# The tail's seven-product feed-forwards: VectorE's order at the entry, TensorE's first products, and the adding up of the banks are rebuilt

## The chip, the cores and the metric

One core of a Trainium2 chip runs the whole program in one launch. The metric is the device time in microseconds of that core, the median of several runs; less is better.

## The reference, cut to what matters

Two transformer blocks of depth 2 follow one another over 256 tokens of width 1024. The change touches the second one, called the tail here, whose two layers (A and B) each end in the same feed-forward and normalisation:

```python
def sq_relu_mlp(x, w1, w2):
    return jnp.square(jax.nn.relu(x @ w1)) @ w2

def layer_norm(x, g, b):
    mu = jnp.mean(xf, axis=-1, keepdims=True)
    var = jnp.mean(jnp.square(xf - mu), axis=-1, keepdims=True)
    ...
...
        x = layer_norm(ALPHA * x + sq_relu_mlp(x, mlp_w1[i], mlp_w2[i]), ln_ffn_g[i], ln_ffn_b[i])
```

`w1` is 1024 x 4096, `w2` is 4096 x 1024, all in f32. ALPHA is the square root of 2.

## The kernel before, in words

**Digits.** Large products are not done on f32 operands. Each operand is split into a high and a low part in the type fp32r. ScalarE writes the high part as a copy (`w_hi`, `hid_hi`, `s_hi`, `t_hi`), VectorE the low part as the f32 value less the high part (`w_lo`, `hid_lo`, `s_lo`, `t_lo`), and TensorE adds up three products (high times low, low times high, high times high).

**Tiles.** The weights of a feed-forward come as 16 tiles of 2 MB: `ff1.0` to `ff1.7` hold 512 columns of `w1` each, `ff2.0` to `ff2.7` the 512 rows of `w2` that go with them. They rotate through three ring buffers, in the order ff1.0, ff1.1, ff2.0, ff1.2, ff2.1 and so on. SyncE loads a tile when TensorE has given its buffer back (`tile_used`). The low part is written over the f32 tile in the ring.

**Seven products.** In A and B, `ff2.0` to `ff2.6` are multiplied with a scheme of seven products in place of eight: activations (two halves of tokens) and weights (two halves of rows, two halves of columns) are combined by sums and differences first. `dve_form_sums` makes four sums of weights (`t_sum`, L1353), `dve_hidden_sums` four sums of activations (L1373 to L1378), `dve_form_lows` the low parts (L1365) in four steps: 0 for the left columns (`col_hi`, shown as w_hi_work), 1 for the right columns (`right_hi`, shown as w_hi_big), 2 and 3 for two of the sums (`t_hi`). `dve_hidden_first` is the low part of the first token half (L1386), `dve_hidden_sums_low` that of the sums (L1398). The seven results grow in seven banks of PSUM over the seven tiles: banks 1 to 7. One of the seven products, that of bank 6, is done in f32 without digits (four matmuls a tile). `ff2.7` is done in the usual way by `ff2(7)`, in four quarters `q` of 12 matmuls each (token half, column half), which land in banks 4 to 7.

**Order on TensorE.** After `ff1(1)`, which makes the hidden blocks 2 and 3 in bank 0 and bank 1, tile `ff2.0` is multiplied: `seven_first(0)`, `seven_second(0)`, `seven_rest(0)`. `seven_first` and `seven_second` are low times high and high times high into banks 4 and 1, and need `hid_lo`; `seven_rest` begins with high times low into the same two banks. Then, for n from 2 to 7: half of `ff1.n` (`ff1_unit(n, 0)`, 48 matmuls), `seven_first(n-1)`, the other half (`ff1_unit(n, 1)`, 48 matmuls), `seven_second(n-1)`, `seven_rest(n-1)`. All units from n = 2 on write bank 0, so each waits until ScalarE has taken the one before out of it (relu, L1317). At the end `ff2(7)`.

**Order on VectorE.** An order written out by hand in `dve_mlp_seven` (L1400): sums of weights, step 0, sums of activations, first low part, step 1, low part of the sums, steps 2 and 3; then for each n the low halves of the next `ff1` tile (`lower_columns`, L1270), and the same again. `dve_seven_products` (L1426) then waits for the last matmul of bank 6 (`seven_done`) and adds the banks into `x` with ten instructions, after which the layer norm (L2959) adds the quarters of `ff2(7)` one by one (L2918) as they come.

**Order on ScalarE.** `act_mlp_seven` (L1309): `hidden(f)` is relu, square and high part of one hidden block (L1317 to L1321), `act_hidden_forms` the high part of the sums (L1307), `act_split` the high parts of the next tile (L1233), `act_column_forms` and `act_right_forms` those of the weights (L1290 to L1302). `form_used` counts four times a tile: TensorE is done with `col_hi`, bank 7, bank 3, bank 2.

**After A**, TensorE turns token half 0 of the normalised `x` (L522) in the last quarter of `ff2(7)`, between its sixth and seventh matmul. After B, the normalised rows are stored and the program ends.

Of the kernel before, what the change touches and what calls it, by code (L numbers as in the profile page):

```python
# [14 lines left out]
P = 128  # L15
S = 256
# [280 lines left out]
def program(nc, ctx, I, out):  # L297
# [169 lines left out]
    hid_turned = sig("hid_turned")  # L467
    t_summed, form_hi, form_lo = sig("t_summed"), sig("form_hi"), sig("form_lo")
    s_summed, s_high, s_low = sig("s_summed"), sig("s_high"), sig("s_low")
    form_used = sig("form_used")  # L470
    seven_done, seven_read = sig("seven_done"), sig("seven_read")
    hid_rows = [hT[:, 2 * t:2 * t + 2, :].rearrange("p k t -> p (k t)") for t in range(TT)]
    ff2_ready, ff2_saved = sig("ff2_ready", 4), sig("ff2_saved", 4)
    stored = sig("stored")
# [14 lines left out]
    def mlp_nth(pre):  # L489

        return 1 if pre == "B." else 0
# [13 lines left out]
    def pe_kit(pe, st, wide_, aux_, tiles, splits, places):  # L505
# [141 lines left out]
        def mlp(pre, turns, between=None, second_token=None, between_at=3, last_turn=None):  # L647
# [91 lines left out]
            def seven_first(n):  # L739

                m, s = seventh(pre, n), 4 * (n % 2)
                pe.wait_ge(form_hi.sem, st.at(form_hi, DIGIT_FORMS * m + 1))
                pe.wait_ge(hid_lo_ready.sem, st.at(hid_lo_ready, FB // 2 * mlp_nth(pre) + 2 * n + 2))
                for o, v in ((bank[4], 1), (bank[1], 0)):
                    if n == 0 and v == 0:
                        pe.wait_ge(wide_.saved.sem, st.at(wide_.saved, wide_.nth_save(f"{pre}f3")))
                    for u in range(2 if v else 1):
                        f = s + 2 * u + v
                        mm(o, hid_lo[:, f, 0:P], col_hi[:, u, v, :], n == 0 and u == 0, False)
                        mm(o, hid_hi[:, f, 0:P], col_hi[:, u, v, :], False, False)  # L750

            def seven_second(n):

# [4 lines left out]
            def seven_rest(n, lo):  # L758

                m, s = seventh(pre, n), 4 * (n % 2)  # L760
                w, first, final = blocks(lo), n == 0, n == LAST - 1
                pe.wait_ge(form_lo.sem, st.at(form_lo, DIGIT_FORMS * m + 1))
                for o, v in ((bank[4], 1), (bank[1], 0)):
                    for u in range(2):
                        mm(o, hid_hi[:, s + 2 * u + v, 0:P], w[:, u, v, 0:BANK], False, final and u == 1 and v == 0)
# [12 lines left out]
                by_digits(bank[3], 1, t_hi[0], t_lo[0], final, form_used)  # L778
                if DIGIT_SUMS > 1:
                    pe.wait_ge(form_lo.sem, st.at(form_lo, DIGIT_FORMS * m + 4))  # L780
                    by_digits(bank[2], 3, t_hi[1], t_lo[1], final, form_used)
                else:
                    pe.wait_ge(t_summed.sem, st.at(t_summed, 4 * m + 3))
                    for u in range(2):
                        mm(bank[2], s_form(sums_, 3, u), t_sum[1][:, u, :], first and u == 0, final and u == 1,
                           form_used if u == 1 else None)
                pe.wait_ge(t_summed.sem, st.at(t_summed, 4 * m + 4))
                for u in range(2):
                    mm(bank[6], hid_f[:, s + 2 * u + 1, P:S], t_sum[2][:, u, :], first and u == 0, False,
                       seven_done if final and u == 1 else None)  # L790

            def seven_open(n):

# [27 lines left out]
            if pre in SEVEN:  # L821
                ff1(1)
                lo = seven_open(0)
                seven_first(0)
                seven_second(0)
                seven_rest(0, lo)
                tile_done()
                for n in range(2, LAST + 1):
                    w = next_columns(f"{pre}ff1.{n}")
                    ff1_unit(n, 0, w)  # L830
                    lo = seven_open(n - 1)
                    seven_first(n - 1)
# [476 lines left out]
    def act_mlp_seven(st, act, wide_, pre, tiles, splits):  # L1309
# [29 lines left out]
        act_split(st, act, tiles, splits, f"{pre}ff2.{LAST}", (0,))  # L1339
        hidden(2 * LAST + 1)  # L1340
        act_split(st, act, tiles, splits, f"{pre}ff2.{LAST}", (1,))

    def dve_form_sums(st, dve, tiles, pre, n):

# [55 lines left out]
    def dve_mlp_seven(st, dve, pre, tiles, splits):  # L1400

        dve_form_sums(st, dve, tiles, pre, 0)
        dve_form_lows(st, dve, tiles, pre, 0, (0,))
        dve_hidden_sums(st, dve, pre, 0)
        dve_hidden_first(st, dve, pre, 0)
        dve_form_lows(st, dve, tiles, pre, 0, (1,))
        dve_hidden_sums_low(st, dve, pre, 0)
        dve_form_lows(st, dve, tiles, pre, 0, range(2, DIGIT_FORMS))
        for n in range(1, LAST):
            ahead = f"{pre}ff1.{n + 1}"  # L1410
            lower_columns(st, dve, tiles, splits, ahead, 0)
# [14 lines left out]
    def dve_seven_products(st, dve, pre):  # L1426

        half = [[x[:, t, c * BANK:(c + 1) * BANK] for c in range(2)] for t in range(TT)]

        def scaled(o, b):  # L1430
            dve.scalar_tensor_tensor(out=o, in0=o, scalar=ALPHA, in1=b, op0=ALU.mult, op1=ALU.add).then_inc(st.up(dve_step), 1)  # L1431

        def added(o, a, b, signal=dve_step):
            dve.tensor_tensor(o, a, b, ALU.add).then_inc(st.up(signal), 1)

        dve.wait_ge(seven_done.sem, st.at(seven_done, mlp_nth(pre) + 1))
        scaled(half[0][1], bank[7])
        scaled(half[1][1], bank[7])
        scaled(half[0][0], bank[1])
        scaled(half[1][0], bank[3])  # L1440
        dve.tensor_copy(y_sum, bank[1]).then_inc(st.up(dve_step), 1)
        dve.wait_ge(st.last.sem, st.reached())
        added(y_sum, y_sum, bank[2])
        dve.wait_ge(st.last.sem, st.reached())
        added(half[0][1], half[0][1], y_sum)
        added(half[1][0], half[1][0], y_sum)
        added(y_sum, y_sum, bank[3])
        dve.wait_ge(st.last.sem, st.reached())
        added(half[1][1], half[1][1], y_sum, seven_read)

    def hidden_pairs(name):

# [2067 lines left out]
```

## Time and profile before

| | |
|---|---|
| median of 3 runs | 1466.64 us |
| the three runs | 1464.3, 1466.64, 1479.1 us |
| the profiled execution's own time | 1466.25 us |
| its span in the profile | 1464.4 us |
| TensorE matmul busy | 1430.8 us (98%) |
| VectorE busy | 953.8 us (65%) |
| ScalarE busy | 772.3 us (53%) |
| GpSimd busy | 289.3 us (20%) |

Times in the profile are from the span's start. The feed-forward of A takes about 985 to 1169 us, that of B 1274 to 1462 us. A matmul's row shows its start and a modelled length; matmuls overlap, so the distance between starts is the cadence. Idle time stands in square brackets behind an instruction, with what ended it.

### The profile page before, as it was taken

To read this page: it belongs to the slowest core of one execution; us is meant where nothing else is said; L and a number is where in the kernel's file an instruction comes from. 1 tells how busy PE (TensorE), PEld (TensorE's weight loads), DVE (VectorE), ACT (ScalarE), POOL (GpSimd) and SP (SyncE) were. 2 spreads that over 40 slices of the span, in tenths; PEclk is the share of its full clock that TensorE was granted. 3 is DMA by queue.
4 is the path that set the end of the run, shared out by engine and by line. 5 is a ranking of instruction groups with operands and counts; after the bars stand their busy time and mean duration, and the time that the engine had idled before them with its cause. 6 is when DMAs were issued, how large, how long until landed. Compare 5 with 4: busy or idle time off the path is not lost.

```text
span 1464.4 us, 20055 instructions
## 1 busy us (share of the span) xinstructions
PE 1430.8 (98%) x8528; PEld 1212.3 (83%) x8528; DVE 953.8 (65%) x1170; ACT 772.3 (53%) x952; POOL 289.3 (20%) x109
## 2 busy tenths in 40 slices
PE   7999999999999999999999999999999999999997
PEld 5788889998877788888989788688888788888886
DVE  5337764454553364854444669878998857589987
ACT  4565626544455554654455366647666336276662
POOL 4598140000029694410000000000000004000000
PEclk9999999999999999999999999999999999999999
DMA  8833345654446543445566353315565453255551
GB/s 303 298 133 127 117 154 192 219 209 176 174 156 235 195 147 116 166 169 212 174 195 219 126 185 112 107 60 182 192 228 176 151 197 115 73 205 187 198 210 49
DMA packets 121224, 250.28 MB, mean 171 GB/s; under 512 B 15040, under 2 KB 27056, under 8 KB 121008
## 3 DMA queue, kind: packets, MB, share of 16 engines
q1 hardware_dynamic: 120872, 248.90, 48.5%
q8 instruction: 68, 1.11, 0.3%
q14 instruction: 20, 0.16, 0.0%
q10 hardware_dynamic: 264, 0.10, 0.0%
HBM read 247.94 MB, written 1.05 MB: 170 GB/s over the span
## 4 chain that ended last, share of the span: by engine, by line
PE 88%; DVE 8%; ACT 2%; POOL 1%; issue 1%; DMA 0%; DVEq 0%; ACTq 0%
PE psum L515 84%; PE psum L522 4%; POOL w_lo L1263 1%; DVE x L2924 1%; DVE w_lo L1270 1%; DVE big L2918 1%; ACT w_hi_big L1299 0%; DVE tiny L2967 0%; DVE x L1431 0%; DMA work<-in_norm_mix 0%; DVE rows L1731 0%; DVE t_lo L1365 0%; DVE w_lo L1365 0%; DVE w_lo L1263 0%; DVE x L2918 0%
## 5 line engine op out<-in xcount | busy, mean ns | idle before, releaser
L515 PE MATMUL psum<-ht_hi,w_lo 128*128 128x256 f32 x960 | 275.6, 287 | 4.9 <-ACT work L1317 3.8
L515 PE MATMUL psum<-w_lo,ht_hi 128*128 128x512 f32 (+1 forms) x576 | 222.4, 389 | 0.9 <-DVE w_lo L1263 0.9
L515 PEld LDWEIGHTS psum<-ht_hi,w_lo 128*128 128x128 f32 x960 | 181.5, 189 | 10.8 <-issue 9.7
L515 PE MATMUL psum<-w_lo,hid_hi 128*128 128x512 f32 x344 | 129.2, 395 | 0.0
L515 PEld LDWEIGHTS psum<-w_lo,ht_hi 128*128 128x128 f32 x576 | 108.3, 188 | 22.4 <-DVE w_lo L1263 1.7
L515 PE MATMUL psum<-ht_lo,w_hi_rows 128*128 128x256 f32 x448 | 126.4, 282 | 0.0
L515 PE MATMUL psum<-ht_hi,w_hi_rows 128*128 128x256 f32 x448 | 126.2, 282 | 0.0
L515 PE MATMUL psum<-ht_lo,w_hi_tmp 128*128 128x256 f32 x448 | 125.1, 279 | 0.0
L515 PE MATMUL psum<-ht_hi,w_hi_tmp 128*128 128x256 f32 x448 | 124.8, 279 | 0.0
L1263 POOL TENSOR_TENSOR w_lo<-ring,w_hi_work 128x2048 fp32r<-128x2048 f32 x12 | 57.4, 4784 | 254.1 <-ACT w_hi_work L1243 254.1
L1243 ACT ACTIVATE w_hi_work<-ring 128x2048 fp32r<-128x2048 f32 x26 | 49.7, 1913 | 81.4 <-PE psum L515 78.8
L515 PE MATMUL psum<-hT,ring 128*128 128x256 f32 (+2 forms) x480 | 89.8, 346 | 0.0
L515 PEld LDWEIGHTS psum<-ht_lo,w_hi_tmp 128*128 128x128 f32 x448 | 85.2, 190 | 3.5 <-issue 2.9
L515 PEld LDWEIGHTS psum<-ht_lo,w_hi_rows 128*128 128x128 f32 x448 | 86.8, 194 | 0.4
L515 PEld LDWEIGHTS psum<-hT,ring 128*128 128x128 f32 (+1 forms) x480 | 78.2, 186 | 10.5 <-issue 2.4
L515 PEld LDWEIGHTS psum<-ht_hi,w_hi_rows 128*128 128x128 f32 x448 | 85.3, 190 | 0.0
L1263 POOL TENSOR_TENSOR w_lo<-ring,w_hi_big 128x2048 fp32r<-128x2048 f32 x3 | 13.7, 4567 | 359.3 <-DVE work L2918 359.3
L515 PEld LDWEIGHTS psum<-ht_hi,w_hi_tmp 128*128 128x128 f32 x448 | 83.9, 187 | 0.0
L515 PEld LDWEIGHTS psum<-w_lo,hid_hi 128*128 128x128 f32 x344 | 64.6, 188 | 15.2 <-issue 0.5
L1529 DVE TENSOR_TENSOR hid_lo<-work,hid_hi 128x512 fp32r<-128x512 f32 x32 | 22.1, 692 | 83.6 <-ACT hid_hi L1503 83.6
L1263 DVE TENSOR_TENSOR w_lo<-ring,w_hi_work 128x2048 fp32r<-128x2048 f32 x15 | 34.4, 2292 | 62.9 <-ACT w_hi_work L1243 62.9
L1263 DVE TENSOR_TENSOR w_lo<-ring,w_hi_tmp 128x2048 fp32r<-128x2048 f32 x24 | 55.0, 2291 | 24.6 <-ACT w_hi_tmp L1243 24.6
(440 smaller groups left out, 3752.0 us busy)
## 6 DMA issues: line engine op xcount, KB each, us to landing
ring<-in_w_ff SPq DMA_DIRECT2D x32, 2048.0 KB, 8.0
ring<-in_mlp_w SPq DMA_DIRECT2D x32, 2048.0 KB, 8.4
ring<-in_w_in SPq DMA_DIRECT2D x19, 2048.0 KB, 7.8
ring<-in_w_out SPq DMA_DIRECT2D x4, 2048.0 KB, 8.1
ring<-in_w_ple_gate SPq DMA_DIRECT2D x4, 2048.0 KB, 8.0
ring<-in_sb_ssm_w_in SPq DMA_DIRECT2D x4, 2048.0 KB, 8.4
ring<-in_dsa_w_in SPq DMA_DIRECT2D x3, 2048.0 KB, 8.0
ring<-in_w_up_nsa SPq DMA_DIRECT2D x2, 2048.0 KB, 8.4
```

The costliest lines, as they stand in the source:

```text
L515: ins = pe.matmul(o, lhsT, rhs, start=start, stop=stop)
L522: ins = pe.transpose(o, in_, ident[0:n, 0:n])
L1243: act.activation(w_hi[place][:, 0:width], ring[n % RING][:, h * width:(h + 1) * width], ACT.Copy) \
L1263: eng.tensor_tensor(w_lo[n % RING][:, c], ring[n % RING][:, c], w_hi[places[name][h]][:, 0:width].bitcast(F32), ALU.subtract) \
L1270: dve.tensor_tensor(w_lo[n % RING][:, :].rearrange("p (k n) -> p k n", k=KT)[:, :, c], ring[n % RING][:, :].rearrange("p (k n) -> p k n", ...
L1529: dve.tensor_tensor(lo, h, hi.bitcast(F32), ALU.subtract).then_inc(st.up(hid_lo_ready), 1)
L2918: return dve.tensor_tensor(o, a, b, op)
L2924: return dve.scalar_tensor_tensor(out=o, in0=a, scalar=s1, in1=b, op0=op0, op1=op1)
```

## The change

It does three things, in A and in B alike:

1. VectorE does steps 1 and 2 of `dve_form_lows` for `ff2.0` ahead of the sums of activations; step 3 stays behind the low part of the sums.
2. `seven_first(0)`, `seven_second(0)` and the first four matmuls of `seven_rest(0)` become `seven_entry`: the same twelve matmuls in another order. Eight that need only `hid_hi` (high times high, high times low) come first, the four that need `hid_lo` last. The wait for ScalarE's relu of hidden block 3 (it frees bank 1) now stands behind the first four.
3. `dve_seven_products` waits per bank (`form_used` 2, 3 and 4) in place of waiting for `seven_done`, which is gone; the copy of bank 1 moves from VectorE to ScalarE (`y_copied`); `seven_read`, for which quarter 3 of `ff2(7)` waits, is signalled after the second instruction in place of the last.

```diff
+            def seven_entry(lo):
+                w, m = blocks(lo), seventh(pre, 0)
+                pe.wait_ge(hid_hi_ready.sem, st.at(hid_hi_ready, FB // 2 * mlp_nth(pre) + 2))
+                pe.wait_ge(form_lo.sem, st.at(form_lo, DIGIT_FORMS * m + 1))
+                for o, v in ((bank[4], 1), (bank[1], 0)):
+                    if v == 0:
+                        pe.wait_ge(wide_.saved.sem, st.at(wide_.saved, wide_.nth_save(f"{pre}f3")))
+                    for u in range(2):
+                        mm(o, hid_hi[:, 2 * u + v, 0:P], col_hi[:, u, v, :], u == 0, False)
+                        mm(o, hid_hi[:, 2 * u + v, 0:P], w[:, u, v, 0:BANK], False, False)
+                pe.wait_ge(hid_lo_ready.sem, st.at(hid_lo_ready, FB // 2 * mlp_nth(pre) + 2))
+                for o, v in ((bank[4], 1), (bank[1], 0)):
+                    for u in range(2):
+                        mm(o, hid_lo[:, 2 * u + v, 0:P], col_hi[:, u, v, :], False, False, form_used if v == 0 and u == 1 else None)
...
-                seven_first(0)
-                seven_second(0)
+                seven_entry(lo)
                 seven_rest(0, lo)
...
+        act.wait_ge(form_used.sem, st.at(form_used, 4 * seventh(pre, LAST - 1) + 2))
+        act.activation(y_sum, bank[1], ACT.Copy).then_inc(st.up(y_copied), 1)
...
         dve_form_sums(st, dve, tiles, pre, 0)
         dve_form_lows(st, dve, tiles, pre, 0, (0,))
+        dve_form_lows(st, dve, tiles, pre, 0, (1, 2))
         dve_hidden_sums(st, dve, pre, 0)
         dve_hidden_first(st, dve, pre, 0)
-        dve_form_lows(st, dve, tiles, pre, 0, (1,))
         dve_hidden_sums_low(st, dve, pre, 0)
-        dve_form_lows(st, dve, tiles, pre, 0, range(2, DIGIT_FORMS))
+        dve_form_lows(st, dve, tiles, pre, 0, range(3, DIGIT_FORMS))
...
-        dve.wait_ge(seven_done.sem, st.at(seven_done, mlp_nth(pre) + 1))
+        used = 4 * seventh(pre, LAST - 1)
+        dve.wait_ge(form_used.sem, st.at(form_used, used + 2))
         scaled(half[0][1], bank[7])
-        scaled(half[1][1], bank[7])
+        dve.scalar_tensor_tensor(out=half[1][1], in0=half[1][1], scalar=ALPHA, in1=bank[7], op0=ALU.mult, op1=ALU.add) \
+            .then_inc(st.up(seven_read), 1)
+        dve.wait_ge(form_used.sem, st.at(form_used, used + 3))
+        scaled(half[1][0], bank[3])
+        dve.wait_ge(y_copied.sem, st.at(y_copied, mlp_nth(pre) + 1))
         scaled(half[0][0], bank[1])
-        scaled(half[1][0], bank[3])
-        dve.tensor_copy(y_sum, bank[1]).then_inc(st.up(dve_step), 1)
-        dve.wait_ge(st.last.sem, st.reached())
+        dve.wait_ge(form_used.sem, st.at(form_used, used + 4))
         added(y_sum, y_sum, bank[2])
...
-        added(half[1][1], half[1][1], y_sum, seven_read)
+        added(half[1][1], half[1][1], y_sum)
+        dve.wait_ge(st.last.sem, st.reached())
```

## Rows read from the trace of the kernel before

**Rows 1.** The page's part 4, the chain that ended last: shares by engine.
```profile
PE 88%; DVE 8%; ACT 2%; POOL 1%; issue 1%; DMA 0%; DVEq 0%; ACTq 0%
```
**Rows 2.** Waits of TensorE, 990 us to the end: total us, times, longest.
```profile
PE psum L515 <- ACT work L1317: 3.8, 2, 1.9
PE psum L522 <- DVE x L2924: 1.9, 1, 1.9
PE psum L515 <- DVE hid_lo L1386: 0.6, 2, 0.3
```
**Rows 3.** Timeline, VectorE, entry of A: start us, length us, instruction, idle before.
```profile
1002.64 2.29 DVE L1365 TENSOR_TENSOR w_lo<-ring,w_hi_work 128x2048 fp32r<-128x2048 f32 x1
...
1008.82 0.42 DVE L1373 TENSOR_TENSOR work<-work 128x256 f32<-128x256 f32 x1 [3.88 <-ACT hid_hi L1463]
...
1014.54 2.35 DVE L1365 TENSOR_TENSOR t_lo<-big,t_hi 128x1024 fp32r<-128x1024 f32 x2
1016.81 2.29 DVE L1270 TENSOR_TENSOR w_lo<-ring,w_hi_tmp 128x2048 fp32r<-128x2048 f32 x1
```
**Rows 4.** Timeline, ScalarE, entry of A.
```profile
1010.53 1.06 ACT L1307 ACTIVATE s_hi<-work 128x1024 fp32r<-128x1024 f32 x1
1011.50 0.58 ACT L1317 ACTIVATE work<-psum 128x512 f32<-128x512 f32 x1
...
1013.32 1.90 ACT L1233 ACTIVATE w_hi_tmp<-ring 128x2048 fp32r<-128x2048 f32 x1
...
1030.49 0.58 ACT L1317 ACTIVATE work<-psum 128x512 f32<-128x512 f32 x1
```
**Rows 5.** Timeline, VectorE, entry of B.
```profile
1292.95 2.29 DVE L1365 TENSOR_TENSOR w_lo<-ring,w_hi_work 128x2048 fp32r<-128x2048 f32 x1
1298.25 0.42 DVE L1373 TENSOR_TENSOR work<-work 128x256 f32<-128x256 f32 x1 [3.01 <-ACT hid_hi L1463]
...
1306.24 2.29 DVE L1270 TENSOR_TENSOR w_lo<-ring,w_hi_tmp 128x2048 fp32r<-128x2048 f32 x1
```
**Rows 6.** Timeline, ScalarE, entry of B.
```profile
1302.74 1.90 ACT L1233 ACTIVATE w_hi_tmp<-ring 128x2048 fp32r<-128x2048 f32 x1
```
**Rows 7.** Timeline, TensorE, entry of A and the first two rounds of its loop.
```profile
1014.68 0.50 PE L515 MATMUL psum<-w_hi_big,s_lo 128*128 128x512 f32 x1 [0.24 <-DVE s_lo L1398]
...
1031.21 0.35 PE L515 MATMUL psum<-ht_hi,w_lo 128*128 128x256 f32 x1 [1.90 <-ACT work L1317]
...
1038.46 0.40 PE L515 MATMUL psum<-w_hi_work,hid_lo 128*128 128x512 f32 x1
...
1054.24 0.28 PE L515 MATMUL psum<-ht_hi,w_lo 128*128 128x256 f32 x1
...
1059.88 0.40 PE L515 MATMUL psum<-w_hi_work,hid_lo 128*128 128x512 f32 x1
```
**Rows 8.** Busy time and granted clock (PEclk) of one stretch after A's wait.
```profile
1033.00:1036.00 3.00, 3.00 (x20) 3.00 (x20) 3.00 (x3) 1.20 (x1) 0.00 (x0) 0.68 0.00 0
```
**Rows 9.** Timeline, TensorE: two other gaps, at the start and at A's end.
```profile
18.14 0.73 PE L515 MATMUL psum<-w_lo,ht_hi 128*128 128x512 f32 x2 [0.94 <-DVE w_lo L1263]
...
1166.14 1.32 PE L522 MATMUL psum<-const,x 128*128 128x128 f32 x8 [1.90 <-DVE x L2924]
```
**Rows 10.** Busy time and granted clock of the stretches behind those two gaps.
```profile
18.00:20.00 2.00, 1.22 (x5) 0.73 (x5) 1.80 (x4) 2.00 (x2) 0.04 (x1) 1.00 1.05 386
...
1168.00:1170.00 2.00, 2.00 (x15) 1.58 (x14) 1.97 (x4) 0.00 (x0) 0.00 (x0) 1.00 0.00 0
```
**Rows 11.** Timeline, VectorE, the ends of A and of B.
```profile
1162.21 0.67 DVE L2918 TENSOR_TENSOR x<-x,psum 128x512 f32<-128x512 f32 x1
...
1438.98 2.29 DVE L1263 TENSOR_TENSOR w_lo<-ring,w_hi_rows 128x2048 fp32r<-128x2048 f32 x1 [1.12 <-ACT w_hi_rows L1243]
1443.96 2.48 DVE L1431 SCALAR_TENSOR_TENSOR x<-x,psum 128x512 f32<-128x512 f32 x4 [2.68 <-PE psum L515]
...
1451.66 0.67 DVE L2918 TENSOR_TENSOR x<-x,psum 128x512 f32<-128x512 f32 x1
```
**Rows 12.** Timeline, TensorE, last matmul of quarter 1 of `ff2(7)`, A and B.
```profile
1159.66 0.40 PE L515 MATMUL psum<-w_hi_rows,hid_hi 128*128 128x512 f32 x1
...
1449.12 0.40 PE L515 MATMUL psum<-w_hi_rows,hid_hi 128*128 128x512 f32 x1
```

More of the change, by code:

```diff
@@ L469, in program @@
     s_summed, s_high, s_low = sig("s_summed"), sig("s_high"), sig("s_low")
-    form_used = sig("form_used")
-    seven_done, seven_read = sig("seven_done"), sig("seven_read")
+    form_used, seven_read, y_copied = sig("form_used"), sig("seven_read"), sig("y_copied")
     hid_rows = [hT[:, 2 * t:2 * t + 2, :].rearrange("p k t -> p (k t)") for t in range(TT)]
@@ L744, in seven_first @@
                 for o, v in ((bank[4], 1), (bank[1], 0)):
-                    if n == 0 and v == 0:
-                        pe.wait_ge(wide_.saved.sem, st.at(wide_.saved, wide_.nth_save(f"{pre}f3")))
                     for u in range(2 if v else 1):
                         f = s + 2 * u + v
-                        mm(o, hid_lo[:, f, 0:P], col_hi[:, u, v, :], n == 0 and u == 0, False)
+                        mm(o, hid_lo[:, f, 0:P], col_hi[:, u, v, :], False, False)
                         mm(o, hid_hi[:, f, 0:P], col_hi[:, u, v, :], False, False)
+            def seven_entry(lo):
[12 more added lines that the diff above has]
+                        mm(o, hid_lo[:, 2 * u + v, 0:P], col_hi[:, u, v, :], False, False, form_used if v == 0 and u == 1 else None)
             def seven_second(n):
@@ L761, in seven_rest @@
                 w, first, final = blocks(lo), n == 0, n == LAST - 1
[L762 to L765, printed above, removed]
+                if not first:
+                    pe.wait_ge(form_lo.sem, st.at(form_lo, DIGIT_FORMS * m + 1))
+                    for o, v in ((bank[4], 1), (bank[1], 0)):
+                        for u in range(2):
+                            mm(o, hid_hi[:, s + 2 * u + v, 0:P], w[:, u, v, 0:BANK], False, final and u == 1 and v == 0)
                 sh, sl, sums_ = s_hi[n % 2], s_lo[n % 2], s_sum[n % 2]
@@ L788, in seven_rest @@
                 for u in range(2):
-                    mm(bank[6], hid_f[:, s + 2 * u + 1, P:S], t_sum[2][:, u, :], first and u == 0, False,
-                       seven_done if final and u == 1 else None)
+                    mm(bank[6], hid_f[:, s + 2 * u + 1, P:S], t_sum[2][:, u, :], first and u == 0, False)
             def seven_open(n):
@@ L1431, in scaled, with added @@
             dve.scalar_tensor_tensor(out=o, in0=o, scalar=ALPHA, in1=b, op0=ALU.mult, op1=ALU.add).then_inc(st.up(dve_step), 1)
-        def added(o, a, b, signal=dve_step):
-            dve.tensor_tensor(o, a, b, ALU.add).then_inc(st.up(signal), 1)
-        dve.wait_ge(seven_done.sem, st.at(seven_done, mlp_nth(pre) + 1))
+        def added(o, a, b):
+            dve.tensor_tensor(o, a, b, ALU.add).then_inc(st.up(dve_step), 1)
+        used = 4 * seventh(pre, LAST - 1)
+        dve.wait_ge(form_used.sem, st.at(form_used, used + 2))
         scaled(half[0][1], bank[7])
-        scaled(half[1][1], bank[7])
+        dve.scalar_tensor_tensor(out=half[1][1], in0=half[1][1], scalar=ALPHA, in1=bank[7], op0=ALU.mult, op1=ALU.add) \
[3 more added lines that the diff above has]
+        dve.wait_ge(y_copied.sem, st.at(y_copied, mlp_nth(pre) + 1))
         scaled(half[0][0], bank[1])
-        scaled(half[1][0], bank[3])
-        dve.tensor_copy(y_sum, bank[1]).then_inc(st.up(dve_step), 1)
-        dve.wait_ge(st.last.sem, st.reached())
+        dve.wait_ge(form_used.sem, st.at(form_used, used + 4))
         added(y_sum, y_sum, bank[2])
```

## The prediction

> **What bounds the kernel now.** I read the chain that ended last first: 88% of it is TensorE [rows 1], so a change on VectorE or ScalarE can only give what TensorE waits for, or what lies behind its last matmul. The second view, TensorE's waits from 990 us to the end, is therefore short and nearly complete [rows 2]: 3.8 us for the relu at L1317 in two waits of 1.9, 1.9 us for the layer norm's last step, 0.6 us for `hid_lo`. In the 474 us of that stretch hardly anything else is to be had.
>
> The timelines then say who stands behind each wait. At A's entry VectorE idles 3.88 us before the sums of activations and has no gap after them [rows 3]; ScalarE's relu at 1030.49 us comes only when VectorE has fed it, and TensorE starts at 1031.21 [rows 4, 7]. B repeats it (idle 3.01 us) [rows 5]. At the ends VectorE idles 2.7 us until the last seven-product matmul, and only then begins ten instructions that most of the banks were ready for [rows 11].
>
> A third view adds a cost that no wait shows. Behind the 1.90 us gap the granted clock is 0.68 over 1033 to 1036 us, partly at the lower of its two levels, 1.2 in place of 2.4 GHz [rows 8]. The 48 matmuls of that unit take 1038.46 - 1031.21 = 7.25 us, those of the next round 1059.88 - 1054.24 = 5.64 us [rows 7]: the lower clock costs 1.6 us in A. B has the same gap, and I take the same price.
>
> **Part 1, steps 1 and 2 of the low parts into the idle time.** One step of the right columns takes 2.2 us (the 2.29 us of the same shape, less the overlap of rows), a step of a sum half of 2.27 us, 1.14 [rows 3]: 3.34 us move.
> - A: step 0 ends at 1004.9 us, so the moved work ends at 1008.3, and the sums still start at 1008.82 [rows 3]. Cost nothing; cover 3.88 us, of which 0.5 is left.
> - B: step 0 ends at 1295.2, the moved work at 1298.5; the sums start 0.25 us later than at 1298.25 [rows 5].
> - Behind the sums VectorE reaches the next tile's low half (L1270) earlier. It was at 1016.81 in A. Now the low part of the sums starts when ScalarE's `s_hi` is done (1010.53 + 1.06 = 1011.6), ends at 1012.8, step 3 at 1013.9. But ScalarE's high half for L1270 is ready only at 1013.32 + 1.90 = 1015.2 [rows 4]. So of 3.34 us only 1016.81 - 1015.25 = **1.56 us** come through. This is what is late next: ScalarE's order, not VectorE's.
> - B: 1302.74 + 1.90 + 0.25 = 1304.9 against 1306.24, **1.33 us** [rows 5, 6].
> - From there to the relu of block 4 the two engines hand work to each other without slack, so the relu and TensorE's restart move by the same amount.
>
> **Part 2, TensorE's order at the entry.** The first product no longer waits for `hid_lo` (0.32 us in each entry, half of 0.6 [rows 2]), and the 0.24 us before 1014.68 goes too, since `s_lo` is ready at 1012.8 [rows 7]. The new wait stands after four matmuls, for the relu of block 3 (1011.50 + 0.58 = 1012.1 [rows 4]); four matmuls at some 0.235 us from 1011.0 end at 1011.9, so it costs 0.2 us in A and, with B's 0.25 us, some 0.4 there. Queued behind it are eight entry matmuls and the whole first tile. TensorE gains about 0.65 us in A and 0.4 in B, and waits them out again at the relu of block 4: worth **nothing** by itself. The order of products within a bank changes no duration.
>
> The gap at that relu becomes 1.90 - 1.56 + 0.65 = 1.0 us in A and 1.90 - 1.33 + 0.4 = 1.0 in B.
>
> **The clock.** No operation in the trace tells what a 1.0 us gap does here; the bounds are no fall (gain 1.6 us each) and the same fall (0). Nearest is the gap of 0.94 us at 18.14, behind which the granted clock stays at 1.00; even A's end with 1.90 us keeps 1.00 [rows 9, 10]. I take no fall: **2 x 1.6 = 3.2 us**. The Trainium skill (TensorE: Matmul & The Clock Gate, "Why this matters for your kernels") lets the clock fall only behind idle stretches longer than any here; by that page the 1.6 us would not be there before, and the sum would come to 6.9 us, or 1459.4. The trace disagrees with it: 0.68 stands behind 1.90 us of idling [rows 8].
>
> **Part 3, the adding up.** Before, ten instructions start at 1443.96 and the layer norm's second addition (quarter 1) at 1451.66 [rows 11]. Now VectorE starts when it has the low half behind it, 1438.98 + 2.29 = 1441.3. Banks 7, 3 and 2 are done by then or within 1 us: behind bank 2 come only four f32 matmuls before 1443.9, and a bank takes six at 0.235 us. ScalarE's copy of bank 1, taken at the relu's 0.58 us for the same shape [rows 4], runs during bank 3; the cover is bank 3's and bank 2's 2.8 us. If that cover is gone, it costs VectorE up to its own old copy, some 0.6 us. Nine instructions at 0.62 to 0.7 us, 5.9 us, end at 1447.2. Before, they ended at 1450.3; 3.1 us are free. Now what is late is quarter 1: its last matmul ends at 1449.12 + 0.40 = 1449.5 [rows 12], so the second addition starts at 1449.56 in place of 1451.66: **2.1 us** of the 3.1 come through at B's end, and the rest of the norm follows unchanged (quarter 3 ends 5.6 us after quarter 1, just ahead of its addition).
> In A the same step moves from 1162.21 to 1159.66 + 0.40 + 0.05 = 1160.1, by 2.1 us [rows 11, 12]. There TensorE's turn is bounded by its own arrival, so the gain is the wait, **1.9 us** [rows 2, 9]. The earlier `seven_read` is hidden: quarter 3 starts at about 1452.3, 2 us after the old signal.
>
> No DMA is issued by a moved step; SyncE's loads follow TensorE and move with it.
>
> **Sum.** 1.56 + 1.33 + 3.2 + 1.9 + 2.1 = 10.1 us against the profiled execution's 1466.25 us (span 1464.4 and 1.85 around it): **1456.2 us**. That execution lies 0.4 us under the median of the runs shown; the runs spread from 1464.3 to 1479.1, so I let 1.5 us stand for the spread.
>
> **Rivals.**
> - *The clock still falls* behind the 1.0 us gaps. For: it fell behind both 1.90 us gaps at this place. Against: [rows 9, 10]. Once: 1457.8; twice: 1466.25 - 6.9 = 1459.4.
> - *The entry gives nothing*, because ScalarE is the bound there, not VectorE: its high halves and the column copies may keep their times. For: half of the moved 3.34 us is already lost to it. Against: between 1015.2 and the relu at 1030.49 ScalarE has less to do than the time holds. Only the ends count: 1466.25 - 4.0 = 1462.3.
> - *Slower.* The moved steps now stand between `hid_hi` and the sums. If ScalarE's right copy came only at the end of the idle time (3.9 us later in A, 3.0 in B), the full 3.34 us would delay `s_hi`, the high halves and the relu: in A 3.34 - 1.56 = 1.8 us lost, in B 3.34 - 1.33 = 2.0, together what the ends give (4.0), with gaps of over 3 us and, if the slow stretch doubles with the gap, 1.6 us more in each: 1466.25 + 3.8 - 4.0 + 3.2 = 1469.3. It decides from about 3 us of lateness. Against: VectorE's step 0 in A starts at 1002.64 without a wait [rows 3]; nothing points to a late copy.
> - *The ends don't move*, since the per-bank signals come with the last one or another instruction holds VectorE: 1466.25 - 6.1 = 1460.1. Against: each signal is tied to its own bank's last matmul.
>
> **Chances.** Forecast 0.57; clock falls once or twice 0.2; entry nothing 0.08; ends don't move 0.06; slower 0.03; the rest a better case, such as an earlier step of ScalarE, or a shifted measurement. The range takes the forecast less 2.7 us (spread, and a clock that stays up elsewhere) and reaches over the clock's case and the entry's: 1453.5 to 1462.5. About 1% (14.7 us) is what a measurement of this kernel can tell from no change; no case but a gain half as large again reaches it. Faster by over 1%: 0.03; within 1%: 0.94; slower by over 1%: 0.03.
>
> **What would show it.** In the changed kernel's trace: L1365 twice more before L1373, whose idle is then under 0.6 us; L1270 some 1.5 us sooner behind L1373 than before; TensorE's wait for L1317 near 1.0 us twice; granted clock 1.00 behind both; no wait at A's L522; L1431 starting some 2.6 us before the last f32 matmul ends, and VectorE waiting for TensorE before quarter 1's addition. The prediction is wrong if the relu's wait keeps 1.9 us, if the clock falls behind a shorter gap, or if a wait at bank 1 of over 0.5 us shows at the entry.

## The result, and the profile after

The changed kernel takes 1456.34 us (median of 20 runs, 1455.5 to 1473.34), the kernel before 1478.82 us beside it (20 runs, 1464.19 to 1496.05); ratio 0.9898, 95% interval [0.9868, 0.9928]. The forecast of 1456.2 us is met to 0.1 us, and still the change in the medians, 22.5 us, is more than twice the 10.4 us that I forecast from the shown 1466.64. That the time itself is met so closely is partly luck: runs of one level spread by some 3 us in either kernel.

The runs, put in order, say why. Those of before fall on levels: nine at 1464.19 to 1466.64, ten at 1478.74 to 1482.91, one at 1496.05. Eighteen runs of the changed kernel lie at 1455.5 to 1458.83, two at 1470.8 and 1473.34. Between the lower levels (medians 1465.5 and 1456.1) lie **9.4 us**; the rest is that 11 of 20 runs of before and 2 of 20 after were on an upper one, so that one median lay up there and the other did not. The profiled execution after is itself an upper one: 1473.34 us, span 1471.2.

**The part that was changed.** TensorE's waits after, from 985 to 1475 us (engine, its line, what it waited for, us in total, times, longest); compare [rows 2]:

```profile
PE psum L514 <- ACT work L1329: 2.4, 3, 1.0
PE psum L514 <- DVE big L2936: 0.6, 1, 0.6
PE psum L521 <- DVE big L2936: 0.6, 1, 0.6
PE psum L514 <- issue: 0.5, 1, 0.5
PE psum L521 <- DVE scr L2945: 0.2, 1, 0.2
```

The relu (now L1329) is waited for 1.0 us twice in place of 1.9, and a third time for 0.3: that is the new wait for bank 1. The waits for `hid_lo` and for the norm's last step are gone. VectorE at A's entry (start, us, line, operation; idle before in brackets):

```profile
1019.55 2.29 DVE L1379 TENSOR_TENSOR w_lo<-ring,w_hi_work 128x2048 fp32r<-128x2048 f32 x1
1021.76 2.29 DVE L1379 TENSOR_TENSOR w_lo<-ring,w_hi_big 128x2048 fp32r<-128x2048 f32 x1
1023.97 1.22 DVE L1379 TENSOR_TENSOR t_lo<-big,t_hi 128x1024 fp32r<-128x1024 f32 x1
1025.74 0.43 DVE L1387 TENSOR_TENSOR work<-work 128x256 f32<-128x256 f32 x1 [0.55 <-ACT hid_hi L1481]
...
1028.54 1.23 DVE L1412 TENSOR_TENSOR s_lo<-work,s_hi 128x1024 fp32r<-128x1024 f32 x1 [0.34 <-ACT s_hi L1319]
1029.69 1.22 DVE L1379 TENSOR_TENSOR t_lo<-big,t_hi 128x1024 fp32r<-128x1024 f32 x1
1032.16 2.29 DVE L1282 TENSOR_TENSOR w_lo<-ring,w_hi_tmp 128x2048 fp32r<-128x2048 f32 x1 [1.26 <-ACT w_hi_tmp L1245]
```

Against [rows 3], the idle time before the sums is 0.55 us in place of 3.88, and the low half of the next tile (L1282) starts 6.42 us behind the sums' start in place of 1016.81 - 1008.82 = 7.99: 1.57 us sooner. It now waits 1.26 us for ScalarE's high half, the bottleneck named in the prediction. TensorE's restarts at the relu in A and B, and the granted clock behind the restarts (last three figures of a window's row: clock, DMA share, GB/s), against [rows 8]:

```profile
1046.57 0.36 PE L514 MATMUL psum<-ht_hi,w_lo 128*128 128x256 f32 x1 [1.02 <-ACT work L1329]
1331.06 0.35 PE L514 MATMUL psum<-ht_hi,w_lo 128*128 128x256 f32 x1 [1.03 <-ACT work L1329]
```

```profile
core 0: us, PE busy (x) PEld busy (x) DVE busy (x) ACT busy (x) POOL busy (x), PEclk, DMA share, GB/s
1048.00:1051.00 3.00, 3.00 (x28) 3.00 (x28) 3.00 (x2) 1.56 (x1) 0.00 (x0) 1.00 0.12 44
1333.00:1336.00 3.00, 3.00 (x28) 3.00 (x27) 3.00 (x3) 1.06 (x1) 0.00 (x0) 1.00 0.06 20
```

VectorE at the end of B, and ScalarE's copy of bank 1, against [rows 11, 12]:

```profile
1447.85 2.29 DVE L1275 TENSOR_TENSOR w_lo<-ring,w_hi_rows 128x2048 fp32r<-128x2048 f32 x1 [1.12 <-ACT w_hi_rows L1255]
1450.06 0.68 DVE L1445 SCALAR_TENSOR_TENSOR x<-x,psum 128x512 f32<-128x512 f32 x1
...
1455.82 0.69 DVE L2936 TENSOR_TENSOR x<-x,psum 128x512 f32<-128x512 f32 x1
1456.54 0.69 DVE L2985 BATCH_NORM_STATS2 tiny<-x 128x6 f32<-128x512 f32 x1
1458.42 0.69 DVE L2936 TENSOR_TENSOR x<-x,psum 128x512 f32<-128x512 f32 x1 [1.19 <-PE psum L514]
```

```profile
1448.30 0.60 ACT L1355 ACTIVATE big<-psum 128x512 f32<-128x512 f32 x1 [0.48 <-PE psum L514]
```

The adding up follows the low half without a gap, and quarter 1's addition now waits 1.19 us for TensorE. From VectorE's step 0 in A (1002.64 before, 1019.55 after) to the same step in B (1292.95, 1304.68) the changed kernel is 5.18 us shorter (forecast for A: 1.56 + 1.6 + 1.9), and from there to quarter 1's addition (1451.66, 1458.42) 4.97 us (forecast for B: 1.33 + 1.6 + 2.1). All 10.1 us of the sum are thus in these two traces.

**The part that was not changed.** The same trace is 15.6 us later than before already at 165 us, in the first layer of the first block. Before, VectorE and then GpSimd at that place:

```profile
113.76 2.07 DVE L1731 TENSOR_TENSOR work<-work,tiny 128x512 f32<-128x512 f32 x1
116.68 4.79 DVE L1731 TENSOR_TENSOR work<-work,const 128x256 f32<-128x256 f32 x2 [0.85 <-ACT work L1606]
...
122.22 0.55 DVE L1734 TENSOR_SCALAR tiny<-tiny 128x16 f32<-128x16 f32 x1
...
123.10 0.37 DVE L1731 TENSOR_TENSOR tiny<-tiny 128x16 f32<-128x16 f32 x1
123.50 1.18 DVE L1731 TENSOR_TENSOR work<-work,tiny 128x512 f32<-128x512 f32 x1
```

```profile
110.64 4.64 POOL L1263 TENSOR_TENSOR w_lo<-ring,w_hi_zb 128x2048 fp32r<-128x2048 f32 x1
115.19 5.11 POOL L1263 TENSOR_TENSOR w_lo<-ring,w_hi_scr 128x2048 fp32r<-128x2048 f32 x1
120.25 8.46 POOL L2069 TENSOR_TENSOR tmp<-big,const 128x256 f32<-128x256 f32 x8
```

After, VectorE, GpSimd, TensorE, and the granted clock of one window:

```profile
113.73 12.23 DVE L1749 TENSOR_TENSOR work<-work,tiny 128x512 f32<-128x512 f32 x1
126.66 1.72 DVE L1749 TENSOR_TENSOR work<-work,const 128x256 f32<-128x256 f32 x2 [0.70 <-ACT work L1624]
...
129.13 4.47 DVE L1752 TENSOR_SCALAR tiny<-tiny 128x16 f32<-128x16 f32 x1
133.64 0.25 DVE L1905 RECIPROCAL tiny<-tiny 128x16 f32<-128x16 f32 x1
133.93 4.13 DVE L1749 TENSOR_TENSOR tiny<-tiny 128x16 f32<-128x16 f32 x1
138.10 0.69 DVE L1749 TENSOR_TENSOR work<-work,tiny 128x512 f32<-128x512 f32 x1
```

```profile
110.72 4.60 POOL L1275 TENSOR_TENSOR w_lo<-ring,w_hi_zb 128x2048 fp32r<-128x2048 f32 x1
115.27 4.62 POOL L1275 TENSOR_TENSOR w_lo<-ring,w_hi_scr 128x2048 fp32r<-128x2048 f32 x1
119.85 5.56 POOL L2087 TENSOR_TENSOR tmp<-big,const 128x256 f32<-128x256 f32 x8
```

```profile
138.89 1.09 PE L521 MATMUL psum<-const,work 128*128 128x128 f32 x4 [13.05 <-POOL w_lo L1275]
```

```profile
130.00:144.00 14.00, 5.11 (x15) 4.17 (x16) 11.86 (x8) 0.80 (x1) 8.03 (x2) 0.51 0.00 0
```

One subtraction takes 12.23 us in place of 2.07. Before, it ended at 115.83, just after GpSimd passed from one instruction to the next (115.19 to 115.28), and that next one took 0.5 us longer. After, it was passed over there and at each of the eight short ones from 119.85 on, nine times, and ended at 125.96, when GpSimd had come to a wait of its own (119.85 + 5.56 = 125.41). Two tiny instructions then take 4.47 and 4.13 us, each beside one long GpSimd instruction. TensorE turns what the chain leaves in `work`: that is ready at 138.79 in place of 124.68. The row names GpSimd, but VectorE's result came last, 0.1 us before the restart. TensorE idles 13.05 us. Its granted clock is 0.51 over 130 to 144 us, most of which it idles; at the lower level it works for the 5.1 us behind the restart. An estimate from these rows: 13.05 us and half of 5.1 make 15.6. The Trainium skill (SBUF — State Buffer, "Who interferes with whom") says that a VectorE instruction with two inputs in SBUF contends with a GpSimd instruction that reads there, and that the order of issue decides which of the two blocks. The trace agrees for the first turn: the GpSimd instruction of 110.72 us was there before the subtraction of 113.73. It shows more besides: the nine that came later went ahead of it too.

### The profile page after: what moved, and what is told of

It reads as the page before. It is cut to its first block, busy times and chain, and to the rows that moved or that the text cites. A ratio compares the mean times of both kernels' runs of the same rounds, so it can differ in the third digit from the quotient of the medians.

```text
span 1471.2 us, 20055 instructions
## 1 busy us (share of the span) xinstructions
PE 1431.1 (97%) x8528; PEld 1211.8 (82%) x8528; DVE 966.2 (66%) x1168; ACT 773.4 (53%) x954; POOL 286.6 (19%) x109
## 4 chain that ended last, share of the span: by engine, by line
PE 86%; DVE 7%; ACT 3%; POOL 2%; issue 1%; DMA 1%; DVEq 0%; ACTq 0%
PE psum L514 83%; PE psum L521 3%; POOL w_lo L1275 2%; DVE work L1749 1%; DVE w_lo L1282 1%; DMA ring<-in_mlp_w 1%; DVE w_lo L1275 1%; DVE big L2936 1%; DVE big L1367 0%; ACT w_hi_big L1311 0%; DMA work<-in_norm_mix 0%; DVE x L2942 0%; DVE rows L1749 0%; DVE w_lo L1379 0%; ACT s_hi L1319 0%
## 5 line engine op out<-in xcount | busy, mean ns | idle before, releaser
L514 PEld LDWEIGHTS psum<-w_lo,ht_hi 128*128 128x128 f32 x576 | 108.8, 189 | 22.5 <-DVE w_lo L1275 1.7
```

Source lines behind the costliest of these rows:

```text
L514: ins = pe.matmul(o, lhsT, rhs, start=start, stop=stop)
```

## The experiments

They ran in four groups on four chips, each beside its own runs of the kernel before. "Lower level" is a run's place within some 6 us of the fastest, "upper" one at 13 us or more above it. "Ratio" is to before on the same chip and goes by means that include upper runs (all but the one at 1488.91 us). Where the two kernels met the upper level in unlike shares, it tells little of the change, and the text below compares the medians of the lower level.

| kernel | runs on lower level: range, median | upper | ratio [95%] |
|---|---|---|---|
| chip 14: before | 23: 1463.1 to 1466.89, 1465.56 | 0 | |
| e1_after_again | 5: 1455.74 to 1457.86, 1456.37 | 0 | 0.9941 [0.9929, 0.9953] |
| e2_dve_order | 5: 1459.68 to 1461.69, 1461.33 | 0 | 0.9969 [0.9957, 0.9981] |
| e3_entry_only | 11: 1459.75 to 1462.84, 1461.41 | 1 | 0.9981 [0.9964, 0.9999] |
| e4_ends_only | 9: 1458.52 to 1463.09, 1460.25 | 3 | 0.9997 [0.9968, 1.0026] |
| chip 4: before | 21: 1464.01 to 1467.02, 1465.82 | 12 | |
| e5_after_pause | 11: 1456.1 to 1459.38, 1456.84 | 0 | 0.9912 [0.9878, 0.9946] |
| e6_before_pause | 12: 1464.18 to 1468.36, 1465.68 | 0 | 0.9976 [0.9946, 1.0005] |
| e7_relu_first | 9: 1452.96 to 1454.9, 1453.82 | 3 | 0.9902 [0.9857, 0.9947] |
| e8_gap_back | 10: 1458.19 to 1463.82, 1461.66 | 2 | 0.9955 [0.9919, 0.9991] |
| chip 8: before | 17: 1464.09 to 1467.51, 1465.67 | 0 | |
| e9_relu_pause | 5: 1453.48 to 1455.13, 1453.89 | 0 | 0.9922 [0.9909, 0.9934] |
| e10_pool_late | 7: 1460.51 to 1461.86, 1461.67 | 0 | 0.9972 [0.996, 0.9983] |
| e11_pe_order | 11: 1463.91 to 1466.88, 1465.96 | 0 | 1.0002 [0.9993, 1.001] |
| e12_after_more | 5: 1456.41 to 1458.38, 1457.83 | 0 | 0.9946 [0.9933, 0.9958] |
| chip 15: before | 15: 1463.95 to 1467.0, 1466.39 | 1 | |
| e13_after_rate | 4: 1455.37 to 1457.46, 1456.89 | 1 | 0.9937 [0.9924, 0.9951] |
| e14_before_again | 11: 1463.91 to 1466.94, 1466.24 | 0 | 1.0 [0.9991, 1.0009] |
| e15_relu_again | 5: 1453.51 to 1455.87, 1454.51 | 0 | 0.9924 [0.9911, 0.9936] |

One further run of before on chip 4, 5211.39 us, is left out everywhere; its cause is not known.

**e1_after_again, e12_after_more**: the changed kernel as it is.

> The changed kernel once more, as a yardstick and to count levels. The runs so far fall on levels some 14 us apart: before 1464 to 1467 and 1479 to 1483 us (and one 1496), after 1455.5 to 1459 and 1471 to 1473. Theory C (chance): the upper level is a stall in the first block, which the change does not touch; it shows here in both kernels at about the same rate, and the lower levels differ by 9 to 10 us. Theory L (the change removes it): the kernel before keeps its upper level in half of its runs, this one nearly never.

> The changed kernel a third time, to count levels beside the kernel before on one chip. Theory C (the level is a chance of the chip and the launch, not of the change): about the rate of the kernel before in this call. Theory L (the change lowers it): before a third or more, this one near none, as in the first 20 runs of each (11 and 2).

Between the lower levels' medians lie 9.2 and 7.8 us. The relu waits are 1.0 us and the clock stays at 1.00 behind them, in both. No run of either kernel, before or changed, was on the upper level on these two chips, so they tell nothing of how often it is met.

**e2_dve_order**: the kernel before with VectorE's order alone.

```diff
+        dve_form_lows(st, dve, tiles, pre, 0, (1, 2))
...
-        dve_form_lows(st, dve, tiles, pre, 0, (1,))
...
-        dve_form_lows(st, dve, tiles, pre, 0, range(2, DIGIT_FORMS))
+        dve_form_lows(st, dve, tiles, pre, 0, range(3, DIGIT_FORMS))
```

> The kernel before with VectorE's new order at the entry alone. My theory: relu's wait down by 1.56 us in A and 1.33 in B, to 0.3 to 0.6 us each, since TensorE is not earlier as in the full change, and no fall of the clock behind it: 2.9 + 3.2 = 6.1 us below the lower level of before. Rival: TensorE's order is what opens the entry, and this alone gives under 1 us.

4.2 us gained between the medians, against 6.1 expected. The relu is waited for 0.8 us twice (0.3 to 0.6 expected), `hid_lo` 0.9 us in all, and the 1.9 us at A's end stay. In the trace VectorE's part is as expected: from the first product of `ff2.0` in A to the restart at the relu of block 4 it is 18.24 us in place of 19.78, so 1.54 us sooner. The traces point to the clock for the missing 1.9 us, since before it does not fall in every execution (see below): against the trace of before, in which it fell behind both relu gaps, this one is 5.9 us shorter from `ff2.0` in A (with the wait ahead of it) to the end.

**e3_entry_only**: the changed kernel with the adding up of before (`seven_done` and VectorE's copy of bank 1 are back).

```diff
-        dve.wait_ge(form_used.sem, st.at(form_used, used + 2))
+        dve.wait_ge(seven_done.sem, st.at(seven_done, mlp_nth(pre) + 1))
```

> Both parts at the entry (VectorE's order and TensorE's), the adding up at the end as before. My theory: 6.1 us below the lower level of before, the same as VectorE's order alone, with waits for the relu of 1.0 us. Rival (TensorE's order counts): over 1 us faster than VectorE's order alone.

1461.41 against e2's 1461.33: TensorE's order is worth nothing here, as the prediction said. As in e2, 4.2 us are gained and not the 6.1 expected.

**e11_pe_order**: the kernel before with TensorE's order alone.

```diff
-                seven_first(0)
-                seven_second(0)
+                seven_entry(lo)
```

> The kernel before with TensorE's new order at the entry alone (eight products that need only the high part first, the wait for bank 1 behind the first four). My theory: the 0.3 us before the first product and part of the 0.24 us before the sums go, and come back at the relu of block 4, whose end VectorE sets: within 0.3 us of before, the relu's wait 0.3 to 0.6 us longer (2.2 to 2.5 us), the clock no better or worse by a little for it. Rival: TensorE gains 0.5 us per entry, 1 us in all.

Nothing in time either, but not as expected: the relu gap did not grow, since TensorE now waits 0.42 us for `s_lo` first, and again in B:

```profile
PE psum L515 <- ACT work L1331: 3.8, 2, 1.9
PE psum L522 <- DVE x L2938: 1.9, 1, 1.9
PE psum L515 <- DVE s_lo L1412: 0.9, 2, 0.4
```

The trace has something else to tell of the clock. It did not fall behind the two relu gaps of 1.89 us, but behind the gap at A's end, which left it at 1.00 in the trace of before [rows 9, 10]:

```profile
1165.83 1.32 PE L522 MATMUL psum<-const,x 128*128 128x128 f32 x8 [1.90 <-DVE x L2938]
```

```profile
1167.00:1171.00 4.00, 4.00 (x17) 2.87 (x16) 3.61 (x7) 0.00 (x0) 0.00 (x0) 0.57 0.00 0
```

**e4_ends_only**: the kernel before with the new adding up alone (the changed lines of `dve_seven_products`, and ScalarE's copy).

```diff
+        act.wait_ge(form_used.sem, st.at(form_used, 4 * seventh(pre, LAST - 1) + 2))
+        act.activation(y_sum, bank[1], ACT.Copy).then_inc(st.up(y_copied), 1)
```

> The adding up of the banks alone, the entry as before. My theory: the wait at L522 in A goes (1.9 to 2.0 us), the second addition in B comes 2.1 us sooner: 4.0 us below the lower level of before; relu's two waits of 1.9 us and the fall of the clock behind them stay. Rival: the parts do not add, as the end gives more or less than 4 us without the entry's gain.

5.3 us gained against 4.0 expected, with both relu waits untouched:

```profile
PE psum L514 <- ACT work L1315: 3.8, 2, 1.9
PE psum L514 <- DVE hid_lo L1386: 0.6, 2, 0.3
```

```profile
1030.00:1034.00 4.00, 3.41 (x29) 3.44 (x30) 4.00 (x3) 3.52 (x4) 0.00 (x0) 1.00 0.36 143
1034.00:1038.00 4.00, 4.00 (x29) 3.67 (x29) 4.00 (x4) 1.44 (x3) 0.00 (x0) 1.00 0.07 6
```

The clock did not fall behind a gap of 1.89 us, nor in B. What stands in [rows 8] is thus one outcome of two. Its nine runs lie at a mean granted clock of 0.994 (1463.09) to 0.999 (1458.52 to 1458.59).

**e8_gap_back**: the changed kernel with two ScalarE copies ahead of the relu of block 4, to widen its gap.

```diff
+        for _ in range(2):
+            act.activation(y_sum, x[:, 0, 0:BANK], ACT.Copy).then_inc(st.up(act_step), 1)
+            act.wait_ge(st.last.sem, st.reached())
```

> The changed kernel with two copies of 128 x 512 on ScalarE ahead of the relu of block 4, which widens TensorE's wait there from 1.0 to some 2.2 us, longer than before the change, and changes nothing else. If a gap of this length brings the clock down: 2.5 us for the copies and up to 3.2 us for the clock, with the fall in some runs and not in others, as in the run with the ends alone (two gaps of 1.9 us, no fall). If the clock is set by something else than the gap: 2.5 us and no fall, or a fall behind the 1.0 us gaps too.

Gaps of 2.35 us, and the clock fell behind both. The lower level's median, 1461.66 us, is 4.8 us above that of e5 on the same chip, of which the two wider gaps are 2.7:

```profile
1034.00:1038.00 4.00, 4.00 (x23) 4.00 (x22) 4.00 (x4) 1.86 (x2) 0.00 (x0) 0.57 0.00 1
1320.00:1326.00 6.00, 5.69 (x35) 5.72 (x36) 6.00 (x5) 3.23 (x4) 0.00 (x0) 0.72 0.13 49
```

**e7_relu_first, e15_relu_again**: the changed kernel with the relu of block 4 ahead of ScalarE's copy of the right columns.

```diff
-        act_right_forms(st, act, tiles, pre, 1)
+        act_right_forms(st, act, tiles, pre, 1, lambda: hidden(4))
```

> The changed kernel with ScalarE's relu, square and high part of hidden block 4 put ahead of the high half of the right columns of tile ff2.1 (and of the second sum's). Theory: the relu's wait of 1.0 us in A and in B is ScalarE's order and goes whole, what is put back (1.9 us later) is not needed by TensorE for another 8 us: 2.0 us under the changed kernel. Rival: the steps put back delay VectorE's low parts and TensorE waits at the rest of tile ff2.1 instead, no gain.

> The changed kernel with ScalarE's hidden block 4 ahead of the high part of the right columns of the second tile (as in the earlier run of it: 9 executions at 1453.0 to 1454.9, three 15 us above). It gives more executions without the pause on GpSimd. Theory 1: upper level in a like share as the kernel before on the same chip. Theory 2: since it holds the whole change, under a tenth. Lower level expected at 1454, that is 2.2 us under the changed kernel.

The waits of 1.0 us are gone, and 2.4 us of time with them (1454.51 against 1456.89 on chip 15; on chip 4 it is 3.0 us, 1453.82 against e5's 1456.84; 2.0 and 2.2 expected): what was left at the relu was ScalarE's order, as the prediction read it.

**e5_after_pause, e6_before_pause**: the changed kernel and the one before, with GpSimd waiting between the two halves of a weight tile of the first block, in both of its layers, until VectorE has written the subtraction's result.

```diff
-                lower_split(st, pool, TILES, SPLITS, "in8")
+                lower_half(st, pool, TILES, SPLITS, "in8", 0)
+                pool.wait_ge(cmp_arg.sem, st.at(cmp_arg, 1))
+                lower_half(st, pool, TILES, SPLITS, "in8", 1)
```

> The changed kernel, with one wait more on GpSimd in the first block: between its two halves of tile in8 it waits until VectorE has done the subtraction that took 12.2 us in the slow run's trace (114 to 126 us). Stall theory: the upper level is that instruction, kept out while GpSimd's instructions follow one another; with the pause VectorE always gets its turn, the subtraction takes 0.7 to 2.1 us in every profile, no run lies on an upper level, and the lower level keeps its 1456 us (the pause is 0.6 us on GpSimd, which is ahead). Rival: the upper level has another cause and stays at its rate of 1 in 5 to 1 in 10, or the pause delays in8 and costs over 1 us.

> The kernel before with the same pause. Stall theory: lower level of before (1464 to 1467 us) and no upper level. Rival: as in the run beside it. Both together add to the count: without the pause 15 of 97 runs of all kernels so far lay 14 us or more above their lower level.

On the chip where kernels without the pause were on the upper level in 17 of 57 runs, those with it never were in 23; chance alone would do that about once in 700. The subtraction takes 2.06 us in e5, and GpSimd's second half waits 0.63 us for it:

```profile
115.99 4.60 POOL L1275 TENSOR_TENSOR w_lo<-ring,w_hi_scr 128x2048 fp32r<-128x2048 f32 x1 [0.63 <-DVE work L1749]
```

**e9_relu_pause**: relu first and pause together.

> The changed kernel with both additions: ScalarE's relu of block 4 put first, and GpSimd's pause in the first block. Both theories held one by one (2.2 us less; no upper level in 23 runs), they touch nothing in common: 1454.2 us, all runs between 1452.5 and 1456.5, no upper level. Rival: the pause costs a few tenths in this arrangement, 1454.6 us.

The best version: 1453.89 us (1454.2 expected), 3.9 us under e12 on the same chip and 2.4 under the changed kernel's first median. None of its 5 runs was on the upper level, but on this chip no kernel was.

**e10_pool_late**: the changed kernel with GpSimd held ahead of that weight tile until VectorE has taken the scores out of PSUM, two steps ahead of the subtraction.

```diff
+                pool.wait_ge(aux.saved.sem, st.at(aux.saved, aux.nth_save("cmp1")))
```

> A pause of GpSimd in another place: the changed kernel, with GpSimd held before its first half of tile in8 until VectorE has taken over the masked scores (about 113 us), so that its two halves and the eight products behind them follow one another without a break while VectorE's subtraction waits. Stall theory (VectorE is kept out by instructions of GpSimd that follow one another): the upper level stays, at the rate of the kernels without a pause or above it, and the subtraction is longer than 2.1 us in the profile. Rival (any shift of GpSimd's timing by 2 us cures it): no upper level, as with the pause between the halves.

The subtraction takes 4.49 us: in this order it waits for one GpSimd instruction (113.12 to 117.74 us, the subtraction 113.80 to 118.29), but gets the turn behind it. The upper level was expected to stay and none of seven runs was on it; on a chip where before had none either that tells little. It costs 3.8 us against e12 on the same chip.

**e13_after_rate, e14_before_again**: both kernels once more, for how often the upper level is met.

> The changed kernel, unchanged. Of its executions so far, 2 of 20 (first result) and 0 of 10 (two further chips) lay some 14 us above the others, of the kernel before 11 of 20, 0 of 23, 12 of 33 and 0 of 17. Theory 1 (the chip sets the rate, the change does not): where a chip shows the upper level at all for the kernel before, the changed kernel shows it in a like share, a third or so of the executions, and its median stays at 1456 to 1458. Theory 2 (the change lowers the rate): the changed kernel shows it in under a tenth while the kernel before shows it in a third or more. On a chip where neither shows it, nothing is told.

> The kernel before, unchanged. Both theories: 1464 to 1467 us on the lower level, 1478 to 1483 on the upper one. It is here for its profiled execution: if that lies on the upper level, the subtraction of GpSimd's neighbour on VectorE in the first block, 2.07 us in the trace of before, should take about 12 us, TensorE should then wait some 13 us for the low part that GpSimd makes, and the granted clock should fall to 0.5 behind that wait. If it lies on the lower level, the subtraction should take 2.1 us.

The profiled execution of e13 took 1488.91 us, and shows the stall twice, once in each layer of the first block: the subtraction, TensorE's clock behind its 13.05 us of idling, and in the second layer the same:

```profile
114.86 12.24 DVE L1749 TENSOR_TENSOR work<-work,tiny 128x512 f32<-128x512 f32 x1
```

```profile
549.79 12.23 DVE L1749 TENSOR_TENSOR work<-work,tiny 128x512 f32<-128x512 f32 x1
```

```profile
130.00:142.00 12.00, 1.97 (x7) 1.81 (x8) 11.79 (x8) 1.94 (x2) 9.05 (x3) 0.50 0.00 0
566.00:580.00 14.00, 5.04 (x15) 4.10 (x16) 11.93 (x8) 0.86 (x1) 8.10 (x2) 0.52 0.01 1
```

Two stalls cost 1488.91 - 1456.89 = 32.0 us, 16 each; the run of before at 1496.05 fits two as well (30.6 above 1465.5). The changed kernel met the level in 1 of 5 runs on a chip where before did in 1 of 27; the theories were about a chip on which before meets it in a third, so neither is tested. The profiled execution of e14 is one of the lower level, and the subtraction takes 2.06 us in it, as expected for that case; no trace shows the kernel before on the upper level. In e14 the clock fell behind both relu gaps of 1.9 us (0.57 over four us behind each).

The start of e13's trace shows a fall too, behind the gap of 0.94 us from which the prediction had argued; here it is 0.93 us, and TensorE is busy for 2.45 of the four us from 16 to 20:

```profile
20.00:24.00 4.00, 3.98 (x11) 3.19 (x12) 3.51 (x2) 1.43 (x2) 4.00 (x1) 0.57 1.08 432
```

## Why the prediction was right, and where it failed

**The step that failed** is the last one of the sum: "the runs spread from 1464.3 to 1479.1, so I let 1.5 us stand for the spread." One run of three 12.5 us above the others is no spread of a single level. It was a second level, and I neither priced it nor asked which of the two a median would come from. What the runs show in its place: a stall of 14 to 16 us in code that the change does not touch, once or twice in an execution, in 24 of 120 runs of before over all chips, and in 11 of the 20 that stand in the result (that before's upper runs are this stall rests on their height and on e6). So the median before lay at 1478.82. With such a level in view, "faster by over 1%" is not a case of 0.03: it comes out whenever the upper level holds half the runs of before and not half of those after.

**VectorE's order**: right. 3.34 us were moved, 1.57 came through in A (1.56 forecast), and L1282 waits for ScalarE. The relu gaps are 1.02 and 1.03 us, 1.0 forecast.

**TensorE's order**: right in sum (e2 equals e3, e11 is nothing). The new wait for bank 1 takes 0.1 us in A and 0.33 in B, 0.2 and 0.4 forecast. What was wrong is a sub-step of e11's expectation, a relu gap of 2.2 to 2.5 us: with TensorE's order alone the time saved at `hid_lo` is waited out in part at `s_lo` (0.42 us in place of 0.24), and the gap keeps 1.89 us.

**The clock**: the mechanism was right, its size on average too large. No fall stands behind the 1.0 us gaps in any of the seven traces that have them (after, e1, e3, e5, e10, e12, e13: 14 gaps). One fall costs 1.5 us, 1.6 forecast: the 48 matmuls of [rows 7] take 7.25 us in before, e6 and e14, where the clock fell, and 5.7 in e4 and e11, where it did not. Where it fell twice the whole sum comes out. From the first product of `ff2.0` in A, with the wait ahead of it, to the end of the span, before takes 453.3, 453.6 and 453.5 us (before, e6, e14) and the changed kernel 443.4 to 443.6 in six traces (after, e1, e5, e10, e12, e13): 10.0 us on average, 10.1 forecast.

Behind the 1.9 us gaps, though, it fell in only three of five traces (before, e6, e14; not e4, e11), and I had charged it in full from one. The mean granted clock that each run lists gives an estimate of its price on average. Of 87 runs of before on the lower level (the first 20 have no such list), 40 have 0.994 (median 1466.57) and 19 have 0.997 (1464.19). The 14 of e1, e12 and e13 have 0.997 (six, 1457.84) or 0.998 (eight, 1456.39). At a like 0.997 the kernels differ by 6.35 us, against 6.9 in the sum without the clock; over all of them the means are 1465.62 and 1456.97, 8.65 apart. That leaves about 2.3 us for the clock in place of 3.2; e2, with 4.2 us gained of which 2.9 are VectorE's, leaves 1.3. These are rough, since a mean clock does not tell where the fall was: behind a gap of 2.67 us ahead of A (at some 935 us in before), which the change does not touch, it fell in 12 of 17 traces and not in e1, e4, e5, e7 and e9, and e11 has a mean of 0.995 without a fall at the relu.

The argument for "no fall" was weaker than I took it for. Its nearest gap, the one at the start (0.94 us in the trace of before), has a fall behind it in three of 17 traces (e8, e13, e15), and A's end with 1.9 us in one of six (e11). That the 1.0 us gaps at the relu never had it rests on their own 14 cases.

**The ends**: right, with quarter 1 late next: the wait of 1.9 us at A's end is gone, and in B the second addition comes 2.1 us sooner. e4's 5.3 us are more than its 4.0 because the clock stayed up more often: four of its nine runs have a mean of 0.998 or 0.999, which none of the 87 of before has, and its trace shows no fall behind any gap named here. At a like 0.997 e4 has 1460.25 and 1460.68, 3.5 to 3.9 under before. Why the clock stayed up more often with the same gaps is not known.

**The rivals**: "entry gives nothing" falls with e2, "ends don't move" with e4, "slower" with the rows of VectorE's entry, since ScalarE's copy was not late (VectorE did the three steps at 1019.55 to 1025.19 us without a wait). "The clock still falls" falls for the gaps of 1.0 us.

**Open**: what brings the upper level, and whether the change makes it rarer. The first runs (11 of 20 against 2 of 20) speak for it. The rest does not: on chip 4, kernels that hold the whole change met it in 5 of 24 runs (e7, e8) and before in 12 of 33, on chip 15 the changed kernel in 1 of 5 and before in 1 of 27, and e4 in 3 of 12 where before had 0 of 23. Three upper stalls were seen in traces, none of them in the kernel before; that its upper runs have the same cause rests on their height and on e6. What decides whether VectorE or GpSimd gets the first turn is not known.

## What to carry to other kernels

Put the runs in order before summing anything: if they fall on levels, forecast from one level, and price separately how often each is met, since it can outweigh the change. Read a clock price from more than one execution, as the same gap can have both outcomes, and compare like stretches of two traces (here from A's entry to the end) to keep the noise ahead of them out. Where a short VectorE instruction on the critical path lies beside a row of GpSimd instructions without a pause, try a wait on GpSimd at that place (here it cost nothing that the runs show).

## What was not expected of the hardware

- A VectorE subtraction of 2.07 us can take 12.23 us beside GpSimd instructions that follow each other without a pause, passed over nine times. With it an execution is some 14 to 16 us longer. How often differs from chip to chip: 0 of 40 runs of before on chips 14 and 8, 12 of 33 on chip 4. With a wait on GpSimd at that place it was not met in 28 runs (e5, e6 and e9), of which the 23 on chip 4 count; without the wait it came there in 17 of 57.
- The same gap has the granted clock fall to its lower level in one execution and not in another. At the relu it fell behind 6 of 10 gaps of 1.9 us, 2 of 2 of 2.35 us and 0 of 14 of 1.0 us; at A's end behind 1 of 6 of 1.9 us; ahead of A behind 12 of 17 of 2.67 us; at the start behind 3 of 17 of 0.94 us or less. The length of a gap alone thus does not tell.
